# A ninth weight buffer in layer 0, earlier first transposes, modulation sums in halves, and a reordered router, in a two-layer attention and mixture-of-experts kernel

## The reference

```python
for layer in range(2):
    mod = silu(c) @ ada_w[layer] + ada_b[layer]            # 6 vectors of 1024
    sh_a, sc_a, g_a, sh_f, sc_f, g_f = split(mod, 6)
    h = rmsnorm(x, norm_attn[layer]) * (1 + sc_a) + sh_a
    if layer == 0:   # differential attention, 8 heads x 2 x 64, causal, relative bias by bucket
        y = diff_attention(h, a_w_qkv, ..., rel_bias)
    else:            # dilated attention: k, v from shared_dilated_kv(x, silu(c) @ kv_ada_w, kv_w);
        y = dilated_attention(h, b_w_q, ..., rel_bias)      # groups (128, 1), (512, 4), (2048, 16)
    x = x + g_a * y
    h = rmsnorm(x, norm_ffn[layer]) * (1 + sc_f) + sh_f
    # router: the best of 4 groups, in it the best 2 of 8 experts; 32 experts of 1024 -> 512 -> 1024
    y = sum over the 2 experts of gate * (silu(h @ w_gate[e]) * (h @ w_up[e])) @ w_down[e]
    x = x + g_f * y
```

## Time and profile before

| | |
|---|---|
| median of three runs | 1756.11 us (1752.01 to 1756.13) |
| the profiled execution | 1758.47 us |
| its span | 1756.7 us, mean PE clock 0.97 |
| PE busy | 1627.9 us (93%) |
| DVE busy | 655.2 us (37%) |
| ACT busy | 374.6 us (21%) |
| POOL busy | 71.2 us (4%) |
| moved by DMA | 523.01 MB, mean 298 GB/s |
| chain of waits: PE / DMA / DVE | 78% / 14% / 4% of the span |
| layer 0: opening and attention, expert stage | to about 397, to about 867 us |
| layer 1: attention, expert stage | to about 1291, to the end |

### The profile page before, as it was taken

One profiled execution on the slowest core, in us unless ns is written; L12 is line 12 of the kernel. 1 busy time (PEld: TensorE's weight loads), 2 busy tenths in 40 slices (PEclk: granted clock), 3 DMA queues, 4 the chain that ended last, 5 costly groups with the idle time before them and its releaser, 6 DMA issues.

```text
span 1756.7 us, 17705 instructions
## 1 busy us (share of the span) xinstructions
PE 1627.9 (93%) x6680; PEld 703.2 (40%) x6680; DVE 655.2 (37%) x1383; ACT 374.6 (21%) x920; POOL 71.2 (4%) x91
## 2 busy tenths in 40 slices
PE   5899999988999997999799999998889999989997
PEld 2345554462333332333244455444453333323332
DVE  2586665352232321323377222224541322322331
ACT  3123344331001010100220244333320101001000
POOL 1100000200000000000000000001100000000000
PEclk9999999989999998999899999998999999999999
DMA  9981823259999999999957112024299999999997
GB/s 353 361 297 60 287 96 145 96 210 375 421 427 388 428 426 427 426 429 415 381 192 251 37 55 90 1 96 148 107 361 424 426 425 426 428 427 426 428 427 287
DMA packets 106314, 523.01 MB, mean 298 GB/s; under 512 B 7862, under 2 KB 46119, under 8 KB 81646
## 3 DMA queue, kind: packets, MB, share of 16 engines
q1 hardware_dynamic: 81120, 485.11, 68.2%
q10 hardware_dynamic: 17118, 17.46, 3.1%
q0 software_dynamic: 7984, 19.20, 3.0%
HBM read 520.83 MB, written 6.37 MB: 300 GB/s over the span
## 4 chain that ended last, share of the span: by engine, by line
PE 78%; DMA 14%; DVE 4%; issue 2%; SPq 1%; ACT 1%; DVEq 0%
PE psum L2241 18%; PE psum L2272 10%; PE psum L1998 10%; PE psum L2287 9%; PE psum L1800 8%; DMA ring<-in_moe_w_down_dram 4%; PE psum L1970 4%; PE psum L1855 3%; DMA ring<-in_ada_w_dram 3%; DMA ring<-in_moe_w_up_dram 2%; DMA HT<-in_moe_w_up_dram 1%; PE psum L2219 1%; DMA XN<-in_moe_w_up_dram 1%; PE psum L2105 1%; PE psum L1829 1%
## 5 line engine op out<-in xcount | busy, mean ns | idle before, releaser
L2241 PE MATMUL psum<-ring,V 128*32 128x512 f32 (+2 forms) x1408 | 337.0, 613 | 24.0 <-DMA HT<-in_moe_w_up_dram 10.4
L2287 PE MATMUL psum<-V,W 128*128 128x512 f32 x448 | 219.3, 615 | 3.7 <-DVE X L1598 1.4
L1598 DVE TENSOR_TENSOR X<-X,psum 128x512 f32<-128x512 f32 x224 | 153.6, 687 | 110.5 <-PE psum L2287 110.4
L2272 PE MATMUL psum<-ring,V 128*64 128x512 f32 (+2 forms) x704 | 190.1, 606 | 3.5 <-DMA ring<-in_moe_w_down_dram 3.1
L2241 PEld LDWEIGHTS psum<-ring,V 128*32 128x32 f32 (+2 forms) x1408 | 110.5, 131 | 194.5 <-issue 194.4
L1141 DVE SCALAR_TENSOR_TENSOR W<-ring,cact,W 128x512 f32<-128x512 f32 (+1 forms) x224 | 138.5, 618 | 7.7
L1030 ACT ACTIVATE V<-psum,modall,scls 128x128 f32<-128x128 f32 x216 | 81.2, 456 | 280.7 <-PE psum L2219 262.4
L2241 PE MATMUL psum<-HT,V 128*32 128x512 f32 (+2 forms) x256 | 119.9, 623 | 14.0 <-DMA XN<-in_moe_w_up_dram 8.5
L2287 PEld LDWEIGHTS psum<-V,W 128*128 128x128 f32 x448 | 72.8, 189 | 149.7 <-DVE X L1598 85.4
L2241 PE MATMUL psum<-XN,V 128*32 128x512 f32 (+2 forms) x272 | 129.0, 629 | 0.6
L1039 ACT ACTIVATE V<-psum 128x512 f32<-128x512 f32 x28 | 16.7, 597 | 501.6 <-PE psum L2250 399.9
(11 more groups left out here) (333 smaller groups left out, 1791.5 us busy)
## 6 DMA issues: line engine op xcount, KB each, us to landing
ring<-in_moe_w_gate_dram SPq DMA_DIRECT2D x44, 2048.0 KB, 23.2
ring<-in_moe_w_up_dram SPq DMA_DIRECT2D x44, 2048.0 KB, 18.8
ring<-in_moe_w_down_dram SPq DMA_DIRECT2D x44, 2048.0 KB, 23.2
ring<-in_ada_w_dram SPq DMA_DIRECT2D x16, 2048.0 KB, 15.5
HT<-in_moe_w_gate_dram SPq DMA_DIRECT2D x10, 2048.0 KB, 20.3
XN<-in_moe_w_up_dram SPq DMA_DIRECT2D x9, 2048.0 KB, 21.1
XN<-in_moe_w_gate_dram SPq DMA_DIRECT2D x8, 2048.0 KB, 26.4
ring<-in_ada_w_dram ACTq DMA_DIRECT2D x16, 1024.0 KB, 5.2
```

Of the source, the lines that this page charges most:

```text
L1598: return dve.tensor_tensor(x3[:, c, cols], x3[:, c, cols], sum_bank(p, hf, c), ALU.add)
L2241: ins = pe.matmul(bank[2 + 2 * i + b][half * w:(half + 1) * w, :], V[:, col:col + w], slot3(x)[:, k, :], start=(k == 0), stop=(k == KC - 1))
L2272: ins = pe.matmul(bank[6 + hf][half * w:(half + 1) * w, :], HIDDEN_T[:, col:col + w], slot3(x, 4)[:, k, hf * HALF:(hf + 1) * HALF], start= ...
L2287: pe.matmul(sum_bank(p, hf, c), PICK[p % 2][:, c * P:(c + 1) * P], Y[:, hf * HALF:(hf + 1) * HALF], start=True, stop=True).then_inc(s["sum ...
```

## The change

It has six parts.

1. **Ninth buffer in layer 0.** T becomes buffer 8 in layer 0's expert stage too, first used as soon as the attention gate's matmul has read it. The feed-forward gate's diagonal moves from T to V (`gf_diag`). So that T can be overwritten, layer 1's table is no longer made in place: ACT copies four 128-wide parts of it from the bias rows into a DRAM tensor `t1_d` at n = 12 of layer 0's loop, and SP loads T from there (2 MB) in layer 1's opening. The masks are now part of the bias rows: the bucket table grows from 896 to 1408 columns, with a third matmul and a third copy. The rewriting of T by DVE and ACT and two loads go.
2. **Early turns.** The first four groups of transposes run before the fourth modulation block is multiplied, into other banks (`TURN_BANKS`); the other four follow the last `mod_reduce`.
3. **Modulation sums in halves.** Two parts at each n up to 6 and at 13 and 18, one part otherwise (before: two up to 8, then one). The row matmuls come after n = 3, 5, 6, 10, 13, 17, 20 and 24 (before 2, 4, 6, 8, 12, 16, 20 and 24), the first two of them right behind the unit. DVE copies units 0 and 1 ahead of the sums instead of behind them.
4. **Squares in halves.** The last chunk's square is done in two halves; the mean of the first half enters the root of the second as its bias. DVE forms that mean ahead of its last output addition.
5. **Logits by chunks.** Of the four matmuls that pick the logits out, the two of the first half no longer wait for the second half.
6. **One-hot ahead of ids.** `FIRST` is formed before DVE waits for the ids and casts them.

```diff
-HOMES = ((0, 1, 2, 5, 4, 3, 7, 6), (1, 2, 3, 4, 0, 7, 5, 8, 6))
+HOMES = ((0, 1, 2, 4, 8, 7, 5, 3, 6), (1, 2, 3, 4, 0, 7, 5, 8, 6))
-FALL = FDIST + 2 * P
+FLATE = 3 * 2 * P
+FALL = FDIST + FLATE
-PARTS_AT = {n: [(3 + n, 0), (3 + n, 1)] for n in range(1, 9)}
-PARTS_AT.update({n: [(12 + (n - 9) // 2, (n - 9) % 2)] for n in range(9, 25)})
+PART_UNITS = [n for n in range(1, 25) for _ in range(2 if n <= 6 or n in (13, 18) else 1)]
+PARTS_AT = {n: [(4 + x // 2, x % 2) for x, at in enumerate(PART_UNITS) if at == n] for n in range(1, 25)}
+TURN_BANKS = (2, 3, 7, 1, 4, 5, 2, 3)
...
# SP, weights of layer 1, behind the last value block
+                        if l == 1 and i == GROUPS - 1:
+                            sp.wait_ge(t1_out, 64)
+                            sp.wait_ge(*expert_used(sm[0], LAST_IN_T))
+                            sp.dma_start(T[:, :], t1_d.rearrange("p h n -> p (h n)")).then_inc(t1_in, 16)
# SP, experts of layer 0
+                    elif first and home == 8 and l == 0:
+                        sp.wait_ge(*sm[0]["gate_pe"](1))
-                        hankel4 = bass.AP(fb_d.tensor, FDIST, [[1, P], [FALL, H], [1, P]])
-                        sp.dma_start(T1_HANKEL.rearrange("p (h s) -> p h s", h=H), hankel4).then_inc(t1_in, 16)
# ACT, loop of layer 0
+                        if n == 12:
+                            act.wait_ge(fb_out, 16)
+                            for i, at in enumerate((0, FDIST, FDIST + 2 * P, FDIST + 4 * P)):
+                                act.dma_start(t1_d[:, :, i * P:(i + 1) * P], bass.AP(fb_d.tensor, at, [[1, P], [FALL, H], [1, P]])).then_inc(t1_out, 16)
# ACT, second norm
-                square(3)
-                root(s["arg2"], s["root2"], 3)
+                act.wait_ge(*s["y_added"](TC if l == 0 else 2 * TC - 1))
+                act.wait_ge(*s["ss2"](3))
+                act.activation(W[:, 1024:1024 + HALF], x3[:, 3, 0:HALF], ACT.Square, accum_out=small[:, 3:4]).then_inc(s["ss2"].sem, 1)
+                act.wait_ge(*s["y_added"](2 * TC))
+                act.activation(W[:, 1024 + HALF:1024 + D], x3[:, 3, HALF:D], ACT.Square, accum_out=small[:, 45:46]).then_inc(s["ss2"].sem, 1)
+                act.wait_ge(*s["arg2"](4))
+                act.wait_ge(*s["ss2"](5))
+                act.activation(small[:, 11:12], small[:, 45:46], ACT.Sqrt, scale=1.0 / D, bias=small[:, 7:8]).then_inc(s["root2"].sem, 1)
# DVE, loop of layer 0
-                        if 1 <= n <= UNITS0 and UNIT[n - 1][0] == "v":
+                        if 1 <= n <= UNITS0 and (UNIT[n - 1][0] == "v" or n <= 2):
                             unit_out(n - 1)
                         for i, part in PARTS_AT.get(n, []):
                             sum_part(i, part)
...
-                        if n - 1 in TILE_OF:
+                        if n - 1 in TILE_OF and n > 2:
                             unit_out(n - 1)
# DVE, output additions
+                    if u == 2 * TC - 1:
+                        mean_square(s["ss2"], s["arg2"], 3)
                     dve.wait_ge(*s["wo_pe"](u + 1))
# DVE, router
-                dve.wait_ge(*s["rank_pe"](3))
-                dve.tensor_copy(eid[:, :], bank[0][:, 0:E]).then_inc(s["eid_ready"].sem, 1)
+                dve.wait_ge(*s["rank_pe"](2))
                 ... first_at, FIRST ...
+                dve.wait_ge(*s["rank_pe"](3))
+                dve.tensor_copy(eid[:, :], bank[0][:, 0:E]).then_inc(s["eid_ready"].sem, 1)
# PE, opening
+                if i == 2:
+                    pe.wait_ge(*sm[0]["xn_ready"](TC))
+                    pe.wait_ge(setup_dve, 6)
+                    for k in range(4):
+                        first_turn(k)
# PE, logits
-                pe.wait_ge(*s["ht2"](KC + KC // 2 + 2))
-                pe.wait_ge(*s["ht2_v"](KC // 2 + 1))
                 for c in range(TC):
+                    if c == 2:
+                        pe.wait_ge(*s["ht2"](KC + KC // 2 + 2))
+                        pe.wait_ge(*s["ht2_v"](KC // 2 + 1))
```

More of the change, by code:

```diff
@@ L107 @@
 N_HALF = 2 * (N_MOD - N_MOD0)
-PARTS_AT = {n: [(3 + n, 0), (3 + n, 1)] for n in range(1, 9)}
-PARTS_AT.update({n: [(12 + (n - 9) // 2, (n - 9) % 2)] for n in range(9, 25)})
-ROWS_AT = {n: (parts[-1][0] - 5) // 2 for n, parts in PARTS_AT.items() if parts[-1][1] == 1 and parts[-1][0] % 2}
+PART_UNITS = [n for n in range(1, 25) for _ in range(2 if n <= 6 or n in (13, 18) else 1)]
+PARTS_AT = {n: [(4 + x // 2, x % 2) for x, at in enumerate(PART_UNITS) if at == n] for n in range(1, 25)}
+ROWS_AT = {n + (n <= 4): ([i for i, half in parts if i % 2 and half][0] - 5) // 2 for n, parts in PARTS_AT.items() if any(i % 2 and half for i, half in parts)}
 PAIRS_F = 4
@@ L154 @@
 LAST_IN_5 = max(i for i in range(MOE_BLOCKS) if HOMES[0][i % len(HOMES[0])] == 5)
+LAST_IN_T = max(i for i in range(MOE_BLOCKS) if HOMES[0][i % len(HOMES[0])] == 8)
 AT = {b: n for n, b in enumerate(ORDER)}
@@ L168, in bucket_table, with late_buckets @@
     bucket = np.where(n < MAX_EXACT, n, np.minimum(large, BUCKETS - 1))
-    out = np.zeros((BUCKETS + 1, FALL), np.float32)
-    out[bucket, np.arange(FALL)] = (dist >= 0)
+    out = np.zeros((BUCKETS + 1, len(dist)), np.float32)
+    out[bucket, np.arange(len(dist))] = (dist >= 0)
     out[BUCKETS] = (dist < 0)
     return out
+def bucket_table():
+    return bucket_rows(np.arange(FDIST) - (P - 1))
+def late_buckets():
+    i = np.arange(2 * P)
+    far = 4 * (i - (P - 1))
+    return bucket_rows(np.concatenate([np.where(i < P, i + 1, -1), np.where((P - 1 - i) % 4 == 0, far, -1), far]))
 def constants():
@@ L801, in _ @@
                         act.wait_ge(*s["xt_pe"](k + 1))
-                        act.activation(ht3[:, k, :], bank[2 + k % 4], ACT.Identity,
+                        act.activation(ht3[:, k, :], bank[TURN_BANKS[k]], ACT.Identity,
                                        bias=mod[:, k:k + 1], scale=scl[:, 0, k:k + 1]).then_inc(s["ht_ready"].sem, 2)
@@ L1713, in _ @@
             pe.matmul(bank[2][0:H, :], rel, V[0:BUCKETS + 1, 4096:4096 + 512], start=True, stop=True)
-            pe.matmul(bank[3][0:H, 0:3 * P], rel, V[0:BUCKETS + 1, 4608:4608 + 3 * P], start=True, stop=True).then_inc(setup_pe, 1)
+            pe.matmul(bank[3][0:H, :], rel, V[0:BUCKETS + 1, 4608:5120], start=True, stop=True)
+            pe.matmul(bank[7][0:H, 0:FALL - 1024], rel, V[0:BUCKETS + 1, 5120:4096 + FALL], start=True, stop=True).then_inc(setup_pe, 1)
             def mod_reduce(i):
@@ L1731, in mod_pair, with first_turn @@
                 ins.then_inc(mod_red, 2)
+            def first_turn(k):
+                for c in range(TC):
+                    ins = pe.transpose(bank[TURN_BANKS[k]][:, c * P:(c + 1) * P], xn3[:, c, k * P:(k + 1) * P], ident)
+                ins.then_inc(sm[0]["xt_pe"].sem, 1)
             for i in range(4):
@@ L1766, in turned_in @@
                             pe.wait_ge(*s["ht_ready"](k + 1))
-                    pe.wait_ge(*s["xn_ready"](TC))
-                    for k in range(KC):
-                        if k >= 4:
-                            turned_in(k - 4)
-                        elif k < 2:
-                            pe.wait_ge(setup_dve, 6)
-                        for c in range(TC):
-                            ins = pe.transpose(bank[2 + k % 4][:, c * P:(c + 1) * P], xn3[:, c, k * P:(k + 1) * P], ident)
-                        ins.then_inc(s["xt_pe"].sem, 1)
+                    pe.wait_ge(mod_part, 4)
+                    for k in range(4, KC):
+                        if k >= 6:
+                            turned_in(k - 6)
+                        first_turn(k)
                     def unit(n):
@@ L1864, in _ @@
                             tile_ms(n - 1)
+                        if n in ROWS_AT and n <= 5:
+                            mod_pair(ROWS_AT[n])
                         if n in TURN_AT and n < TAIL:
@@ L1874, in _ @@
                             step_scores(STEP_AT[n])
-                        if n in ROWS_AT:
+                        if n in ROWS_AT and n > 5:
                             mod_pair(ROWS_AT[n])
@@ L2173, in _ @@
                 for i in range(2):
-                    ins = pe.matmul(bank[5 + i], ones, ga_diag[l][:, 4 * i:4 * i + 4, :], start=True, stop=True)
+                    ins = pe.matmul(bank[5 + i], ones, gf_diag[:, 4 * i:4 * i + 4, :], start=True, stop=True)
                 ins.then_inc(s["gate_pe"].sem, 1)
```

52 lines of the change are left out of this document (20 added, 32 removed).

## The result

The changed kernel takes 1745.3 us (median of 11 runs, 1742.8 to 1747.7) beside 1755.7 for the kernel before in the same rounds (11 runs, 1748.8 to 1757.2). The ratio is 0.9948, 95% interval 0.9937 to 0.9958: 9 us faster, with the whole interval beyond the 0.3% that can be told. The profiled execution took 1744.6, span 1742.8; before's had a span of 1756.7. These two spans lie 13.9 us apart, the medians 10.4, and the ratio makes 9.1.

A forecast was written before the change was run, and what follows sets the result against it. DMA at about 427 GB/s bounds the expert stages, PE the attentions, modulation blocks and DVE's sums the opening. Terms -1.9 - 10.5 - 1.0 + 0 = -13.4 us gave 1742.7, say 1743; range 1737 to 1751.

The forecast's parts named there:

- narrower band of the forecast: Whole kernel: a time of 1740 to 1746.5 us, given a chance of 0.48.
- signs of being wrong: Layer 0 stage's end moves by under 8 or over 17 us, or layer 1 alone differs by more than 1.
- Opening, -1.9: Layer 0's first units: the 6.97 us gap goes, a new 5.2 us wait comes; net -1.9 us at n = 7.
- Unit 0's start: Opening, early turns: unit 0 starts 2.2 us sooner, 42.7 to 40.5, with bounds 0 and 2.9.
- It buys nothing alone: Opening: the earlier start of unit 0 gains nothing by itself, as the modulation block at 57.69 comes late next.
- ACT's copies, hidden: Layer 0, n = 12: four copies take 4 x 0.43 = 1.7 us to issue, within about 8 us free.
- all four issues stay under 1 us: Sign for ACT's copies at n = 12: each of the four issues takes under 1 us.
- Router of layer 0: Layer 0's router: PE's chain -1.35 us, the weight stream's -0.4.
- Ring, -10.5 with the router and -1.0 at the end: Layer 0's expert stage: ninth buffer and router give -10.5 us, the first of the last four down blocks -1.0.
- no stop at 550: Layer 0's expert stage: the DMA shortfall at 550 to 558 (3.2 us) goes with the ninth slot.
- Layer 1's router, 0: Layer 1's router: reciprocal +0.65 us, one-hot -0.65, PE -0.1, ids +0.85; taken as 0 (-0.8 to +0.9).
- The sum: Whole kernel: -1.9 - 10.5 - 1.0 + 0 = -13.4 us, to 1742.7, say 1743.

The follow-up runs named there:

- experiment 6: The changed kernel with all eight input turns together again behind the fourth modulation block: 1747.1 us, ratio 0.9953 to the kernel before.
- experiment 4: The changed kernel with the copies of units 0 and 1 behind the modulation sum again: 1755.7 us, ratio 1.0005 to the kernel before.
- experiment 1: The changed kernel with layer 0's expert ring back at eight slots in the old order: 1753.2 us, ratio 0.9990 to the kernel before.
- Experiment 8: The changed kernel, but in layer 1 DVE waits for the first half's square behind the last output addition: 1742.6 us, ratio 0.9927 to the kernel before.
- experiment 10: The changed kernel with ACT's four copies at n = 12 made twice, into a second unread tensor: 1755.6 us, ratio 1.0001 to the kernel before.
- experiment 7: The changed kernel with the third row matmul behind unit 7, DVE's mix and copy ahead of its half sum: 1738.2 us, ratio 0.9910 to before.

## Why the prediction was right, and where it was not

The forecast was 1743 and the measurement 1745.3, inside the range and inside the narrower band of the forecast; the layer 0 stage ends where it was said to (842.48 for "near 843"). One of its own signs of being wrong did come: layer 1 alone differs by more than 1 us. Point by point:

- **Opening, -1.9.** Right to a tenth or two as a sum of steps: unit 3 at 64.4 (64.32), sum 9 from 95.1 to 101.1 (its last seven instructions 95.65 to 101.1), a wait of 5.2 (5.14), 2.6 of lower clock (0.87 + 1.76), and -2.2 at n = 7. Following one engine's queue by its durations, instruction for instruction, found the wait that took the gap's place. Unit 0's start was sized wrongly (41.33, I said 40.5), without effect. "It buys nothing alone" fits the trace badly once the gap is gone (experiment 6), though the times leave it open. The order of copy and row matmul, which I priced as one, is a pair (experiment 4).
- **ACT's copies, hidden.** Right that it is hidden, wrong why. I took the short issue of 0.43 us for all four; two took 0.62 and 0.68 and the rest held ACT 3.53, the last one alone 2.39. What hid it is the 4.19 us of the earlier trace rows, not a short queue. The forecast that all four issues stay under 1 us failed. The fit that the prediction takes from the Trainium skill ("DMA: Bandwidth & Descriptors", "Anatomy of one DMA") is given there for DMAs issued by GpSimd. These were issued by ACT, and in the trace of the change the four landed 5.0 to 9.8 us after their issue.
- **Router of layer 0.** Ids -0.4 as forecast; the one-hot matmuls gain 1.6 without the clock where I had 1.35. The two logit matmuls beside the wait gave 0.45 of it, not 0.1.
- **Ring, -10.5 with the router and -1.0 at the end.** The long wait comes 9.3 us sooner, counted from the ids (experiment 1), which with 0.4 for the ids is 9.7 of 10.5. From there to the stage's last wait it is 0.65 more, for my 1.0. Both parts are there: the third block by 389, and no stop at 550. The weak spot is the size of the stop: DMA still falls to 407 GB/s from 426 to 450. A block would be worth 5.9 us, an estimate from the 358 GB/s of the Trainium skill ("DMA: Bandwidth & Descriptors", "Where 436 GB/s comes from"); the trace again moves 426 to 431 GB/s from 450 to 535 and from 550 to 690, and the measurement decides.
- **Layer 1's router, 0: the step that failed.** The reciprocal did come later than before, as the mechanism said (the wait before the last turns grew by 0.54, I had 0.65), and the one-hot's 0.65 was there. But I priced the longer wait by its length alone. Behind it PE's clock falls to its lower level for the 16 logit matmuls (1.55 us more, of which 0.43 is won back because two of the four matmuls that pick the logits out run sooner), and again from the rank matmuls on (1.65 more). With the wait and the one-hot it adds up: 0.54 + 1.55 - 0.43 + 1.65 - 0.65 = 2.66, for the +2.6 measured. Experiment 8 takes the longer wait away, and both slow stretches go with it. Why the second one, behind a wait that has not changed, goes with the first is not shown.
- **The sum.** The spans differ by 13.9 where I had 13.4, but that agreement is in good part luck. Between the points named the two traces also differ by stretches of lower clock in code that the change leaves as it was: 1.4 us for the change between 283 and 335, 0.6 in layer 0's rank matmuls, 2.1 between the last wait of layer 0 and layer 1's router, and 1.4 against it in the last 15 us. For the last two the waits ahead differ as well (3.18 us for 3.95, and 3.04 for 2.34), so a part of them may come of the change; no run separates that. Another 1.5 for it within layer 1's experts I did not follow. The times give the effect without such luck: 10.4 us by the medians and 9.1 by the ratio, 3 to 4 less than forecast. Of that the layer 1 step is 2.6, the ring 0.8 (9.7 for 10.5) and the stage's end 0.35 (0.65 for 1.0).

## What to carry to other kernels

Move a gap only together with what its end is chained to: here a copy moved ahead of a sum gave 4 us alone, leaving it behind when its partner had moved cost 10, and moving the partner one unit further gave another 7. When a wait ahead of a run of short matmuls grows, price the slower clock behind it too, from rows of the same kernel on either side of that length. And where a ring is fed by one DMA stream that sets the pace, as here, count the stops of the stream from the first free choice on, and order the slots by when they are free: a stop of nearly 3 us at its start cost 2.9 at its end.

## What the runs showed of the hardware

- ACT's queue took about three DMAs of 1024 rows of 512 bytes; then each issue held the engine 1.7 to 4.8 us. The first three of eight took 0.62, 0.68 and 1.10 us, the fourth to eighth 14.6 together (experiment 10).
- A wait longer by half a microsecond (1.74 for 1.20 us) went with 3.5 us for the same 16 matmuls in place of 2.01; twelve traces of thirteen fit (the exception, experiment 7, had 1.74 and 2.01).
- From the trace of one of these kernels to that of another, the same instructions behind the same wait ran at another clock: layer 0's eight rank matmuls took anything from 1.08 to 1.92 us behind a wait of 2.43, and from them to the one-hot matmuls two traces differ by up to 2 us. There is one trace of each kernel, so the difference of two spans is no better than a few us.
